# Weight sums of the seven-product pairs made by accumulating transfers, with a fifth weight buffer

## What is computed

```python
def second_block(x, ...):
    ...
        x = x + rms_norm_2(mix, norm_mix_post[l])
        hn = rms_norm_2(x, norm_ffn_pre[l])
        f = (jax.nn.silu(hn @ w_gate[l]) * (hn @ w_up[l])) @ w_down[l]
        x = x + rms_norm_2(f, norm_ffn_post[l])
```

## Time and profile before

| | |
|---|---|
| median of 3 runs | 2551.7 us (2551.49 to 2552.24) |
| the profiled execution's own time | 2553.57 us |
| its span in the profile | 2551.6 us |
| TensorE's mean granted clock, as a share of full speed | 0.996 |
| PE busy | 2507.5 us (98% of the span) |
| DVE busy | 1953.6 us (77%) |
| ACT busy | 1301.3 us (51%) |
| read from memory | 574.15 MB, 226 GB/s |

### The profile page before, as it was taken

One profiled execution on the slowest core, in us unless ns is written; L12 is line 12 of the kernel. 1 busy time (PEld: TensorE's weight loads), 2 busy tenths in 40 slices (PEclk: granted clock), 3 DMA queues, 4 the chain that ended last, 5 costly groups with the idle time before them and its releaser, 6 DMA issues.

```text
span 2551.6 us, 30234 instructions
## 1 busy us (share of the span) xinstructions
PE 2507.5 (98%) x11312; PEld 2050.9 (80%) x11312; DVE 1953.6 (77%) x2508; ACT 1301.3 (51%) x1803; POOL 3.9 (0%) x11
## 2 busy tenths in 40 slices
PE   7999999999999999999999999999999999999998
PEld 6788877788878888888888888888877778888786
DVE  8999999999877777557675677666679894578975
ACT  4435687764554444444444545554555454455543
POOL 0000000000000000000000000000000000000000
PEclk9999999999999999999999999999999999999999
DMA  9998566888945656665655554445444555454473
GB/s 385 356 352 324 210 229 226 284 303 315 364 179 210 231 212 237 241 233 214 215 214 199 197 184 180 165 181 199 171 159 167 209 203 211 168 198 181 178 267 116
DMA packets 80788, 578.23 MB, mean 227 GB/s; under 512 B 9166, under 2 KB 9462, under 8 KB 10881
## 3 DMA queue, kind: packets, MB, share of 16 engines
q1 hardware_dynamic: 79056, 567.25, 60.7%
q10 hardware_dynamic: 1074, 6.37, 0.7%
q0 software_dynamic: 512, 2.69, 0.3%
HBM read 574.15 MB, written 3.70 MB: 226 GB/s over the span
## 4 chain that ended last, share of the span: by engine, by line
PE 76%; DVE 13%; DMA 4%; issue 3%; ACT 3%; SPq 0%; DVEq 0%; ACTq 0%
PE bank L917 71%; DVE wlo L1852 6%; PE bank L890 2%; DMA raw<-in_w_gate 2%; DMA raw<-in_w_in 2%; DVE raw L1862 1%; ACT whi L1241 1%; DVE FT L2384 1%; DVE cv L2085 1%; DVE raw L2303 1%; DMA aside<-in_w_in 1%; PE bank L820 1%; ACT PR L1241 1%; DVE cv L1843 0%; DVE PART L1935 0%
## 5 line engine op out<-in xcount | busy, mean ns | idle before, releaser
L1852 DVE TENSOR_TENSOR wlo<-raw,whi 128x1024 fp32r<-128x1024 f32 x902 | 1091.7, 1221 | 474.9 <-ACT whi L1241 468.9
L1241 ACT ACTIVATE whi<-raw 128x1024 fp32r<-128x1024 f32 x902 | 934.8, 1056 | 832.2 <-PE bank L917 543.3
L917 PE MATMUL bank<-whi,HTh 128*128 128x512 f32 x2376 | 649.2, 395 | 11.4 <-ACT HTh L1241 4.6
L917 PE MATMUL bank<-wlo,HTh 128*128 128x512 f32 x2376 | 638.7, 390 | 1.7 <-DVE wlo L1852 1.5
L917 PE MATMUL bank<-whi,HTl 128*128 128x512 f32 x2376 | 638.4, 390 | 0.0
L917 PEld LDWEIGHTS bank<-whi,HTh 128*128 128x128 f32 x2376 | 439.8, 188 | 108.8 <-ACT whi L1241 12.0
L917 PEld LDWEIGHTS bank<-wlo,HTh 128*128 128x128 f32 x2376 | 445.6, 188 | 99.0 <-DVE wlo L1852 5.7
L917 PEld LDWEIGHTS bank<-whi,HTl 128*128 128x128 f32 x2376 | 447.2, 188 | 95.1
L1862 DVE CUSTOM_DVE_ANT_0 raw<-raw,GT,VECS 128x2048 f32<-128x2048 f32 x95 | 222.6, 2345 | 0.8 <-DMA raw<-in_w_ada 0.4
L917 PE MATMUL bank<-wlo,ACTh 128*128 128x512 f32 x704 | 189.5, 389 | 0.0
L917 PE MATMUL bank<-whi,ACTh 128*128 128x512 f32 x704 | 189.5, 389 | 0.0
(11 more groups left out here) (282 smaller groups left out, 1522.3 us busy)
## 6 DMA issues: line engine op xcount, KB each, us to landing
raw<-in_w_in SPq DMA_DIRECT2D x126, 1024.0 KB, 4.9
raw<-in_w_ada SPq DMA_DIRECT2D x95, 1024.0 KB, 6.5
raw<-in_w_gate SPq DMA_DIRECT2D x88, 1024.0 KB, 5.0
raw<-in_w_up SPq DMA_DIRECT2D x88, 1024.0 KB, 4.8
raw<-in_w_down SPq DMA_DIRECT2D x88, 1024.0 KB, 4.8
raw<-in_w_o SPq DMA_DIRECT2D x16, 1024.0 KB, 7.5
raw<-in_w_out SPq DMA_DIRECT2D x16, 1024.0 KB, 4.8
raw<-in_w_attn_out SPq DMA_DIRECT2D x8, 1024.0 KB, 6.4
```

Source lines behind the costliest of these rows:

```text
L917: i = e.matmul(bank[2 * ch.st + t][:, :], (xl if ps == 1 else xh)[:, k, tk(t)], (lo if ps == 2 else hi)[:, j * 512:j * 512 + 512], start=c ...
L1241: return e.activation(dst, src, ACT.Copy, scale=scale)
L1852: e.tensor_tensor(lo, src, r32(hi), S_).then_inc(lo_done, 1)
```

## The change

- `join` is gone from DVE. GpSimd (POOL) instead issues a transfer for each of the 40 sums: it reads the second half (0.5 MB) from memory once more and adds it to what lies in the star buffer (`accum_op`). It waits for the star's own load and, where an earlier form used the same raw half, until ACT and DVE have split that form.
- The sum is now an addition throughout, so signs move: the combinations `S32`, a negated copy of one activation block for form 1 (`NAh`, `NAl`, two small ACT activations), and one subtraction in place of an addition at the end of a gate chunk.
- `forms_left` begins at slot 11 instead of 15, in five steps of two operations, and waits for the activations' first half only; `forms_high` begins at slot 13 instead of 16.
- `DUO`: form 4 goes from place 9 to 11, form 2 from 11 to 13, form 3 from 13 to 15; forms 1, 5, 6 and 7 stay at 1, 3, 5 and 7. Gate's last piece is form 2, at place 13.
- The array `GT` becomes a fifth raw buffer from `ffn10` on, once PE has done everything before it. Each star is loaded where it is first needed in the plan.

```diff
-FORMS = {1: Form((0, 0), None, 1, 1, ("A", 0, 0)),
+FORMS = {1: Form((0, 0), None, 1, 1, ("N",)),
          2: Form((0, 1), None, 0, 0, ("A", 0, 1)),
          3: Form((1, 1), None, 1, 0, ("S", 3)),
-         4: Form((0, 0), ((0, 1), (0, 0)), 0, 1, ("A", 1, 1)),
-         5: Form((0, 0), ((1, 0), (0, 0)), 1, 0, ("S", 0)),
-         6: Form((0, 0), ((1, 1), (0, 0)), 1, 1, ("S", 1)),
-         7: Form((1, 0), ((1, 1), (1, 0)), 1, 1, ("S", 2))}
-DUO = ["g", 1, "g", 5, "g", 6, "g", 7, "g", 4, "g", 2, "u", 3, "u", "u", "u", "u", "u"]
+         4: Form((0, 0), (0, 1), 0, 1, ("A", 1, 1)),
+         5: Form((0, 0), (1, 0), 1, 0, ("S", 0)),
+         6: Form((0, 0), (1, 1), 1, 1, ("S", 1)),
+         7: Form((1, 0), (1, 1), 1, 1, ("S", 2))}
+DUO = ["g", 1, "g", 5, "g", 6, "g", 7, "g", "g", "u", 4, "u", 2, "u", 3, "u", "u", "u"]
...
-        star = [unit(side, STAR) for side in range(2)]
-        self.stars.update(star)
+        star = {}
...
+                for a in (0, 1):
+                    if a not in star and (a == side or what == 5):
+                        star[a] = unit(a, STAR)
+                        self.stars.add(star[a])
...
+    raw.append(GT[:, :].rearrange("p (a b) -> p a b", a=4))
...
+        if i == P.extra:
+            free.append(NRAW)
...
+            elif place.get(i) == NRAW:
+                w.wait_ge(pe_done, M["ffn10"])
...
         def forms_high(n):
+            q = 4 * STAR
+            w.wait_ge(*part_act[2 * n](7))
+            w.wait_ge(*(g_dve[2](7) if n else m_dve("lo", 6)))
+            for name, dst, src in (("nh", NAh, HTh), ("nl", NAl, HTl)):
+                e.activation(dst[:, :, :], r32(src[:, q:q + 2, tk(0)]), ACT.Copy, scale=-1.0).then_inc(*s_act[n].one(name))
+            yield 2
             w.wait_ge(*s_dve[n]("j"))
             copy(SH[:, :, :], S32[:, :, :]).then_inc(*s_act[n].one("hi"))
...
-            lane.begin((B0, B2)[n] + 16, forms_high(n))
+            lane.begin((B0, B2)[n] + 13, forms_high(n))
...
-                    e.tensor_tensor(SNP[:, i, :], B, SNP[:, i, :], A_).then_inc(emptied["DVE"], 1)
+                    e.tensor_tensor(SNP[:, i, :], B, SNP[:, i, :], A_ if ch.kind == "up" else S_).then_inc(emptied["DVE"], 1)
...
-        def join(p):
-            (ua, ha), (ub, hb) = P.pieces[p].add
-            dst = raw_of(P.pieces[p].unit, P.pieces[p].half)
-            arrived(w, ua)
-            arrived(w, ub)
-            if add_no[p] > 1:
-                w.wait_ge(add_done, add_no[p] - 1)
-            e.tensor_tensor(dst, raw_of(ua, ha), raw_of(ub, hb), S_).then_inc(add_done, 1)
...
-            lane.begin((B0, B2)[n] + 15, forms_left(n))
+            lane.begin((B0, B2)[n] + 11, forms_left(n))
...
+        for p in adds:
+            pc = P.pieces[p]
+            arrived(w, pc.unit)
+            for q in R(p - 1, p - 19, -1):
+                if (P.pieces[q].unit, P.pieces[q].half) == (pc.unit, pc.half):
+                    w.wait_ge(hi_done, q + 1)
+                    w.wait_ge(lo_done, q + 1)
+                    break
+            u, half = P.units[pc.add[0]], pc.add[1]
+            src = A[u.src]
+            e.dma_start(raw_of(pc.unit, pc.half), bass.AP(src.tensor, src.offset + u.off + 1024 * half, [[2048, 128], [1, 1024]]),
+                        accum_op=ALU.add).then_inc(add_no[p][0], 16)
```

More of the change, by code:

```diff
@@ L81, in __init__ @@
         self.last_of = {}
-        self.stars, self.in_duo = set(), set()
+        self.stars, self.in_duo, self.extra = set(), set(), None
     def ada(self, queue, n):
@@ L153, in duo @@
                 ch, (side, half) = chs[f.side], f.raw
-                add = f.add and tuple((star[a], b) for a, b in f.add)
+                for a in (0, 1):
+                    if a not in star and (a == side or what == 5):
+                        star[a] = unit(a, STAR)
+                        self.stars.add(star[a])
+                add = f.add and (star[f.add[0]], f.add[1])
                 pc = Piece(star[side], half, 2, 512, ch, range(4 * STAR + 2 * half, 4 * STAR + 2 * half + 2), what, add)
@@ L241, in make_plan @@
             p.cols(ch, "w_out_2", c + d, range(2, 4), 4)
+    p.extra = len(p.units)
     plan_ffn(p, 1, "_2")
@@ L406, in build @@
     SL = at("SL", 75776 + 2048 * 4, [4, T], f32r)
+    NAh = at("NAh", 49152, [2, 128], f32r)
+    NAl = at("NAl", 74752, [2, 128], f32r)
     u2T = at("u2T", 32768, [8, 2 + T])
@@ L455, in build @@
     S = nc.alloc_semaphore
-    raw_in = [S(f"raw{i}_in") for i in range(NRAW)]
+    raw_in = [S(f"raw{i}_in") for i in range(NRAW + 1)]
     aside_in = [S(f"aside{i}_in") for i in range(len(ASIDE))]
@@ L543, in build @@
     d_items = [(p, c) for p, c in f_items if (p, c) != (0, 0)]
-    add_done = S("add_done")
-    s_act = {n: steps(f"s{n}_act", ["hi"]) for n in DUOS}
+    add_done = [S(f"add{i}_done") for i in R(2)]
+    s_act = {n: steps(f"s{n}_act", ["nh", "nl", "hi"]) for n in DUOS}
     s_dve = {n: steps(f"s{n}_dve", [*"abcdefghij", "lo"]) for n in DUOS}
@@ L590, in build @@
     place, turns, freed_by = {}, {}, {}
-    free, pinned, holder = deque(range(NRAW)), deque(), [[] for _ in range(NRAW)]
+    free, pinned, holder = deque(range(NRAW)), deque(), [[] for _ in range(NRAW + 1)]
     for i in range(len(P.units)):
@@ L623, in build @@
     adds = [p for p in range(NP) if P.pieces[p].add]
-    add_no = {p: i + 1 for i, p in enumerate(adds)}
+    add_no = {}
+    for side in R(2):
+        for i, p in enumerate([p for p in adds if FORMS[P.pieces[p].form].raw[0] == side]):
+            add_no[p] = (add_done[side], 16 * (i + 1))
     closing = {}
@@ L733, in build @@
     WIDE = M["kiwi"]
-    JOIN = AHEAD + 3
     GT_SLOT = [M["conv"] + 6, M["down01"] - 2]
@@ L798, in build @@
     for p in R(NP):
-        for unit in [P.pieces[p].unit, *(a for a, _ in P.pieces[p].add or ())]:
-            final_piece[unit] = p
+        final_piece[P.pieces[p].unit] = p
     def arrived(w, i):
@@ L882, in form @@
                 left = [[x[:, f.left[1], j * 128:j * 128 + 128] for j in R(2)] for x in (SH, SL)]
+            elif f.left[0] == "N":
+                w.wait_ge(*s_act[n]("nl"))
+                left = [[x[:, j, :] for j in R(2)] for x in (NAh, NAl)]
             else:
@@ L1246, in split @@
             if p in add_no:
-                w.wait_ge(add_done, add_no[p])
+                w.wait_ge(*add_no[p])
             if p in home:
@@ L2269, in forms_left @@
             w.wait_ge(*res_act[2 * n](3, 1) if n else part_act[0](15))
-            w.wait_ge(*(g_dve[2](15) if n else m_dve("lo", 14)))
-            w.wait_ge(*part_act[2 * n](15))
-            e.tensor_tensor(s1, h10, h11, A_).then_inc(*d.one("a"))
-            e.tensor_tensor(s3, h00, h10, S_).then_inc(*d.one("b"))
-            w.wait_ge(*d("a"))
-            e.tensor_tensor(s1, s1, l10, A_).then_inc(*d.one("c"))
-            w.wait_ge(*d("b"))
-            e.tensor_tensor(s3, s3, l00, A_).then_inc(*d.one("d"))
-            w.wait_ge(*d("c"))
-            e.tensor_tensor(s1, s1, l11, A_).then_inc(*d.one("e"))
-            w.wait_ge(*d("d"))
-            e.tensor_tensor(s3, s3, l10, S_).then_inc(*d.one("f"))
-            w.wait_ge(*d("e"))
-            e.tensor_tensor(s2, s1, h00, S_).then_inc(*d.one("g"))
-            yield 1
-            w.wait_ge(*d("g"))
-            e.tensor_tensor(s2, s2, l00, S_).then_inc(*d.one("h"))
-            w.wait_ge(*d("h"))
-            e.tensor_tensor(s4, h01, s2, S_).then_inc(*d.one("i"))
-            w.wait_ge(*d("i"))
-            e.tensor_tensor(s4, s4, l01, A_).then_inc(*d.one("j"))
-            yield 2
+            w.wait_ge(*(g_dve[2](7) if n else m_dve("lo", 6)))
+            w.wait_ge(*part_act[2 * n](7))
+            for name, out, a, b, op, after in (
+                    ("a", s1, h10, h11, S_, None), ("b", s3, h10, h00, S_, None), ("c", s1, s1, l10, A_, "a"),
+                    ("d", s3, s3, l10, A_, "b"), ("e", s1, s1, l11, S_, "c"), ("f", s3, s3, l00, S_, "d"),
+                    ("g", s2, h00, s1, S_, "e"), ("h", s2, s2, l00, A_, "g"), ("i", s4, h01, s2, S_, "h"),
+                    ("j", s4, s4, l01, A_, "i")):
+                if after:
+                    w.wait_ge(*d(after))
+                e.tensor_tensor(out, a, b, op).then_inc(*d.one(name))
+                if name in "bdfhj":
+                    yield 1
             w.wait_ge(*s_act[n]("hi"))
@@ L2577, in vector @@
                 pieces_ahead(s)
-            if s + JOIN in add_no:
-                join(s + JOIN)
         for q in R(1, 4):
```

## The result

The change makes the kernel slower: 2595.25 us median of 4 runs (2590.87 to 2595.8) against 2551.97 of the kernel before on the same chip, a ratio of 1.0165 with a 95% interval of 1.0147 to 1.0183. The forecast of 2541.0 missed in sign, and the time lies 8 us above its range.

A forecast was written before the change was run, and what follows sets the result against it. PE, busy 98%, was taken as the bound, so only its 19.2 us lost in pairs could be won; 8.5 would stay through the chain of sums, a gain of 10.7, giving 2541.0 us, whole range 2532 to 2587.

The forecast's parts named there:

- chain of sums: Sums 5 and 6 share a half buffer, so PE waits 2L-11.0 us before form 6 in each pair, 2L-8.5 in the first.
- L: Time from POOL's issue of a sum to its landing; taken as 5.8 us, between ends of 3.3 and 7.3.
- What could be won: Ten pairs of the second network: windows sum to 437.2 us against 418.0 stall-free, so 19.2 us at most.
- rival A: Everything is won: L below 4.3, no pair waits, 2532.5 us; chance 0.08.
- The first pair: Additions and ACT's copy come earlier, so `SL` is there well before form 5 and the 8.4 us loss goes.
- Loads: At pairs' starts, ACT's wait for the first gate unit goes, and so should the other 10.8 us; fifth buffer's load hidden.
- 20L-107.5: Loss staying over all ten pairs, in us, for L above 5.5; a microsecond of L is worth 20.
- rival B: The chain eats the gain: L 6.1 to 6.6, 14 to 25 us stay, time within 5 us of 2551.7; chance 0.17.
- POOL issues sum 5 at -4.1: Counted from PE's place 0 of a pair: `low` of form 1 starts at -5.44, takes 1.22, then POOL issues.
- Behind the waiting split on ACT: While ACT waits for a sum, only the next two pieces' splits stand behind, none wanted sooner than a copy after.
- rival C: Slower, second read paid in full: L 7.3, 19.3 to 34.7 us slower, 2578 us given; chance 0.27.
- D: Starved descriptor writing, or an adder far below a copy's rate: L over 8, time over 2590 us; chance 0.10.

The follow-up runs named there:

- e10: e9's order, with the loads of two plain up units held until sum 5 and sum 7 of the pair have landed; 2591.35 us, ratio 1.0154.
- e12: The changed kernel with the 16 transposes of a pair's left output at four a slot from the second slot on; 2622.74 us, ratio 1.0277.
- e1: The changed kernel with its 40 sums back on DVE in place of the adding transfers; 2534.03 us, ratio 0.9926.
- e6: The kernel before, sums on DVE, plus the change's 40 adding transfers into an array that nothing reads; 2552.73 us, ratio 1.0001.
- e3: The changed kernel with plain copies in place of the adding transfers, so the sums are left out; 2540.83 us, ratio 0.9952.
- e13: e9 with the pair's transposes at four a slot from the second slot on, as in e12; 2567.66 us, ratio 1.0062.
- e2: The changed kernel with a gate piece more ahead of form 5 and one ahead of form 6; 2589.37 us, ratio 1.0144.
- e9: The changed kernel with one gate piece from behind form 7 moved between forms 5 and 6; 2599.91 us, ratio 1.0187.

## Why the prediction was wrong

The forecast was 54.2 us too low. What failed is the wait for the chain of sums, which it put at 2L-11.0, 0.6 us in each pair and the same in all, and its price, which it put at one microsecond per microsecond. Measured were 2.4 to 6.9 us of waits per pair, at 1.56 each. In the forecast's own terms, with 8.5 us left of the losses, the miss adds up like this:

| term | forecast | measured | us |
|---|---|---|---|
| L in the formula | 5.8 | 6.35 | 11.0 |
| POOL issues sum 5 | -4.1 | -3.1 at best | 9.0 |
| late starts and loads on sums | nothing | what is left of 40.3 idle | 11.8 |
| slow running after waits | nothing | 22.4 | 22.4 |

The first two lines come from the formula. The 22.4 is PE's busy time above 418.0. The 11.8 is a remainder, and no run has it by itself; e10 and e12 show what it is made of.

- **What could be won: right.** 19.2 us in the pairs, 418.0 without them; e1's ten windows sum to 418.0, and its 2534.03 us lies 1.5 above the 2532.5 of rival A. *The first pair* and *Loads*: right in the mechanism (no wait for `SL`, no wait at a pair's start, in any kernel with the change's order).
- **DVE, ACT, traffic at no cost: right.** e6 puts the traffic below 3 us; the busy share of the DMA engines rose to 0.66 to 0.73 in the windows, where 0.63 was worked out.
- **L = 5.8: too low, by little.** It is 6.3 us in an undisturbed pair, between my ends of 3.3 and 7.3, and above 6.3 is one of the signs that I gave for a wrong forecast. With L at 6.35 the formula's 20L-107.5 gives 19.5 us, no change in time, rival B. So L alone does not make the change slower. (At 6.3 the formula gives 18.5 and not the 19.2 that stand there; the deciding point is 6.34.) Read as 4.3 us for a plain transfer and 1.5 for the second read, 5.8 had both too low: e3 has 4.5, and 1.9 for the addition.
- **"POOL issues sum 5 at -4.1": wrong, the first step that failed.** Two small terms are missing from it. `low` of form 1 cannot start at -5.44, since the split ahead of it waits for PE's high part of the piece four earlier (in e13's second pair that split starts at 1900.78, which is -6.07), and so ends 0.5 us later than I had it; and POOL issues 0.57 us after the `low` it waits for. That makes -3.1, as e12 and e13 have it in nine pairs. (The first pair's 2.5 us of delay were right but for the same lag: -1.1.) PE's wait per pair is then 2L-10.0, 2.7 us at 6.35; e12's waits for `whi` there are 2.3 to 2.8. Nine more microseconds of waits. (POOL's lag stands before sum 6 as well, and the 0.4 us that I added for `wlo` did not come, but for 0.15 in one pair; the two about cancel.)
- **"Behind the waiting split on ACT stand the splits of the next two pieces; none is wanted sooner than a copy after it": wrong, the second step.** What stands behind is all that ACT and DVE have to do: a set-aside copy, evictions, transposes, silus. The transposes piled up and put sum 5 of the next pair up to 3 us later (e12 removes that), there it met a load (e10), and in other orders the copy itself held PE up (e2, e12). I checked the pieces in the queue behind the wait, and not the other work.
- **"The loads fall at -1.4, 8.1 and 13.6, mostly between the sums": wrong when late.** With sum 5 at -1.4 or later, from the second pair on, the load falls right behind it, 2.3 us more each time (two pairs of the change, six of e9).
- **The price of a wait: left out of the sum, the largest term.** 40.3 us of idle time came with 22.4 us of slow running, so a wait costs 1.56 of itself; I had 1.4 from one pair, and used it for one pair in rival C alone. The windows of before had it: 437.2-425.57, or 11.6 us, of idle time to 19.2 lost, 1.65. In the rows, two matmuls right behind form 6's wait of 5.28 us take 1.22 us, the level of 1.2 GHz, as form 5 did before.
- **The rivals.** C had the right sign, at 27%, and that is in part luck: it had it by L = 7.3, which did not come, and with the measured L its sum gives no change. Its mechanism, the cost of the second read, is there, but makes 11 of the 54 us, and its upper end of 2587 was too low. D's time came about without its L. As for the rates, adding transfers moved 205 GB/s from memory and 205 to 218 from SBUF, copies 314 to 410. The rule that the Trainium skill gives (Collectives: The Full Stack, The bandwidth ceiling: an addition reads two sources on one ring and runs at about half the rate) agrees with these rates, 0.50 to 0.65 of a copy's. The formula of the Trainium skill (DMA: Bandwidth & Descriptors, Anatomy of one DMA) has nothing for an addition, and the estimate of 3.2 us by it is also below e3's plain copy, 4.5.

What was not tried: whether the addition on SP's queue would be issued and land sooner, and whether the transposes could go where neither the sums nor the copies are held up.
